# Five of the first eight expert weights issued in one block behind the output projection of a mixer and expert layer

## The reference

```python
h = rmsnorm(x, g_norm1) * (1 + sc1) + sh1
x = x + gt1 * hybrid_mixer(h, ...)             # ends with  concatenate(...) @ w_out
h = rmsnorm(x, g_norm2) * (1 + sc2) + sh2
x = x + gt2 * moe(h, router_w, router_b, exp_w1, exp_w3, exp_w2)
return rmsnorm(x, g_final)

# moe: softmax of h @ router_w, 2 of 32 experts for each row, then for each expert
ys = (silu(xb @ w1[e]) * (xb @ w3[e])) @ w2[e]
```

## Time and profile before

| | us |
|---|---|
| median of 3 runs | 1104.49 (1103.25 to 1107.17) |
| the profiled execution's own time | 1103.69 |
| its span in the trace | 1101.9 |
| PE busy | 968.8 (88%) |
| DVE busy | 551.5 (50%) |
| ACT busy | 350.6 (32%) |
| all transfers | 295.82 MB, mean 268 GB/s |

### The profile page before, as it was taken

One profiled execution on the slowest core, in us unless ns is written; L12 is line 12 of the kernel. 1 busy time (PEld: TensorE's weight loads), 2 busy tenths in 40 slices (PEclk: granted clock), 3 DMA queues, 4 the chain that ended last, 5 costly groups with the idle time before them and its releaser, 6 DMA issues.

```text
span 1101.9 us, 12838 instructions
## 1 busy us (share of the span) xinstructions
PE 968.8 (88%) x4972; PEld 668.9 (61%) x4972; DVE 551.5 (50%) x848; ACT 350.6 (32%) x515; POOL 132.5 (12%) x131
## 2 busy tenths in 40 slices
PE   3799999999999799983999999999899989988810
PEld 2477888888889488872666546554554455444500
DVE  2588634523662256654873535453543354334547
ACT  5521024323222344322742425222423142234212
POOL 2000000001200002103031112020100102000112
PEclk9899899999999999985999999999999999999965
DMA  9829511111303263357989999999999999998665
GB/s 369 296 88 343 194 40 39 39 39 40 116 2 134 77 259 124 115 162 191 377 326 364 401 428 426 428 427 427 426 427 427 426 426 413 418 426 362 253 243 225
DMA packets 52271, 295.82 MB, mean 268 GB/s; under 512 B 10841, under 2 KB 23146, under 8 KB 35826
## 3 DMA queue, kind: packets, MB, share of 16 engines
q1 hardware_dynamic: 43634, 274.00, 63.0%
q0 software_dynamic: 7424, 16.80, 4.0%
q10 hardware_dynamic: 1152, 4.19, 0.9%
HBM read 278.03 MB, written 25.33 MB: 275 GB/s over the span
## 4 chain that ended last, share of the span: by engine, by line
PE 64%; DMA 19%; DVE 8%; ACT 4%; issue 2%; DVEq 1%; POOL 1%; SPq 0%; ACTq 0%; POOLq 0%
DMA place_dt_float<-in_exp_w_dram 14%; PE bank L1134 7%; PE bank L1115 7%; PE bank L1110 4%; PE bank L817 4%; PE bank L812 4%; PE bank L814 4%; PE bank L813 4%; PE bank L818 3%; PE bank L819 3%; PE bank L1104 3%; DVE place_dt_float32r L1928 3%; PE bank L1107 3%; PE bank L1140 2%; PE bank L986 2%; PE bank L992 2%
## 5 line engine op out<-in xcount | busy, mean ns | idle before, releaser
L1928 DVE TENSOR_TENSOR place_dt_float32r<-place_dt_float,place_dt_float32r 128x4096 fp32r<-128x4096 f32 x32 | 141.4, 4420 | 72.4 <-ACT place_dt_float32r L1398 72.4
L1398 ACT CAST place_dt_float32r<-place_dt_float 128x4096 fp32r<-128x4096 f32 x32 | 115.6, 3613 | 168.4 <-DMA place_dt_float<-in_exp_w_dram 146.8
L1115 PE MATMUL bank<-place_dt_float,tail_dt_float 128*64 128x512 f32 x512 | 113.4, 595 | 2.3 <-DMA place_dt_float<-in_exp_w_dram 2.3
L1134 PE MATMUL bank<-place_dt_float,arena 128*128 128x512 f32 x256 | 113.7, 597 | 1.7 <-issue 1.7
L713 POOL DMA_INDIRECT y_dram<-arena,slot_i x24 | 54.1, 2255 | 440.6 <-DVE arena L1939 440.6
L817 PE MATMUL bank<-low_r 128*128 128x256 f32 (+1 forms) x320 | 93.7, 293 | 0.0
L819 PE MATMUL bank<-low_r 128*128 128x256 f32 (+1 forms) x320 | 90.8, 284 | 0.0
L818 PE MATMUL bank<-low_r 128*128 128x256 f32 (+1 forms) x320 | 90.7, 284 | 0.0
L629 POOL TENSOR_TENSOR stats<-stats,half 128x1 f32<-128x1 f32 (+1 forms) x34 | 31.1, 918 | 467.7 <-DVE stats L1444 440.9
L1104 PE MATMUL bank<-place_dt_float32r,tail_dt_float32r 128*128 128x512 f32 x256 | 71.2, 422 | 15.4 <-ACT place_dt_float32r L1398 12.6
L812 PE MATMUL bank<-low_r 128*128 128x512 f32 x192 | 78.3, 408 | 5.0 <-DVE arena L1553 3.8
(11 more groups left out here) (263 smaller groups left out, 1510.5 us busy)
## 6 DMA issues: line engine op xcount, KB each, us to landing
place_dt_float<-in_exp_w_dram SPq DMA_DIRECT2D x96, 2048.0 KB, 28.3
arena<-in_w_ada_dram SPq DMA_DIRECT2D x24, 1024.0 KB, 9.3
low<-in_w_in_dram SPq DMA_DIRECT2D x11, 1024.0 KB, 5.6
arena<-y_dram SPq DMA_DIRECT2D x3, 2048.0 KB, 16.9
arena<-in_x_dram SPq DMA_DIRECT2D x2, 2048.0 KB, 12.3
wout_dt_float<-in_w_out_dram SPq DMA_DIRECT2D x2, 2048.0 KB, 8.0
arena<-in_x_dram SPq DMA_DIRECT2D x8, 512.0 KB, 3.5
x_dram<-arena SPq DMA_DIRECT2D x8, 512.0 KB, 3.9
```

The lines of the kernel that those rows point to most:

```text
L1115: mm = pe.matmul(out_[rows_, :], x[:, k, rows_], w[:, k, :], start=(k == 0), stop=(k == KD - 1))
L1134: mm = pe.matmul(bank[5 + j][:], hT_sb[:, k, :], ws[0][:, k, cols], start=(k == 0), stop=(k == KF - 1))
L1398: act.copy(part_hi[0 if kind == "w1" else 1], alias[F32][n % SLOTS]).then_inc(S["w_hi"], 1)
L1928: TT(alias[F32R][n], alias[F32][n], part_hi[j].bitcast(F32), ALU.subtract).then_inc(S["w_lo"], 1)
```

## The change

Units 6 and 7 are issued right behind units 3, 4 and 5, so that one loop issues the five. The wait for the gather of pass 1 (`gath[1]`), behind which they stood, is gone, and the load of the gate row `gt2` now stands behind all five. Nothing else is changed.

```diff
             sp.wait_ge(S["out_mm"], 2 * TILES)
             assert all(stream[n][2] < FIXED for n in range(SLOTS))
-            for n in range(3, 6):
+
+            for n in range(3, SLOTS):
                 load_unit(n, stream[n][2])
             for h in range(2):
                 sp.wait_ge(x2_st[h], 32 * TH)
             sp.dma_start(gt2, broad(gate_dram[1:2, :])).then_inc(S["gt_ld"], 16)
-
-            sp.wait_ge(gath[1], 16)
-            for n in range(6, SLOTS):
-                load_unit(n, stream[n][2])
-
             sp.wait_ge(S["order_ready"], 1)
```

## The result

The change makes the kernel slower: a median of 1109.41 us (10 runs, 1108.51 to 1113.21) against 1105.22 us before (10 runs, 1102.10 to 1107.67). The ratio is 1.0045, with a 95% interval of 1.0031 to 1.0058, that is +5.0 us (3.4 to 6.4) on 1105. The forecast was 1108.9 us, with a range of 1104.0 to 1112.0 and a slip of 4.4 us.

A forecast was written before the change was run, and what follows sets the result against it. PE bounds the expert stage first, the weight stream its end. Removed wait 0, plus 4.4 (larger of gather 0's 4.4 and the gate row's 3.7), plus 0: 1108.1 from 1103.69, written as median 1108.9 us; range 1104.0 to 1112.0.

The forecast's parts named there:

- What bounds the stage: Expert stage: PE bounds it first, the weight stream at its end; the chain's first wait for a weight begins at 751.90.
- Removing the wait for gather 1 is worth 0: Units 6 and 7 issued before 519.20: no gain, since PE needs them tens of us later; other end -9.8 us.
- The third set of list writes is not delayed: List writes landing at 509.3, before gather 0: weights are in flight already, so more queued behind add 0.
- Gather 0 from 4.5 to 8.9 us: Gather 0, issued at 514.10 amid weights, lands at 523.0: +4.4 us, judged from gather 3; bounds 0 and +5.5.
- the 1.1 us taken off for its last packets: Gather 0's landing: 524.1 by gather 3's price, cut to 523.0 because its last packets have the engines to themselves.
- Gate row at 524.3 and hidden: Gate row behind all five units lands at 524.3, beside gather 0's larger slip, there when PE has transposed at 525.1.
- a floor of 3.7 us: Before DVE's first `x_evac`: the late gate row alone delays the first product about 3.7 us, even with a quick gather.
- My sign for the loads: Sign expected in the changed profile: DMA busy without a gap to 521, then idle until unit 8 near 535.
- Gathers pass in one go: Rival at gather 0: its packets go together, little delayed, so the gate row binds; +3.7 us, 1108.2; 8%.
- Hidden slip: Rival from the first product to the end: the stream catches up in gaps, absorbing part; +0 to +3 us; 17%.
- Full stream's price: Rival: gather 0 takes 11.8 to 15.7 us, or list writes stretch unit 7's tail; +7.3 to +11.2 us; 12%.
- The clock at the first products: PE's granted clock at the first products: low before and would be after, so 0 us.

The follow-up runs named there:

- late run: Kernel before, with units 6 and 7 issued behind the first product of pass 0 in place of gather 1; ratio 0.9991 to before.
- gate row between: The change, but with the gate row load between units 5 and 6 and not behind all five; ratio 1.0053 to before.
- halves: The change, with units 6 and 7 each loaded as two DMAs of half the columns (8 KB packets, not 16 KB), gate row last; ratio 1.0069 to before.
- none early: Kernel before, with units 3 to 7 all behind the wait for gather 1 and only the gate row ahead; ratio 1.0015 to before.
- two early: Kernel before, with only units 3 and 4 ahead of the gate row, units 5 to 7 behind gather 1; ratio 0.9987 to before, 0.9989 when repeated.
- one unit: Kernel before, with only unit 6 joining units 3 to 5 and unit 7 staying behind gather 1; ratio 1.0013 to before.
- halves with the gate row between: The change, with units 6 and 7 as two half-column DMAs each and the gate row between units 5 and 6; ratio 1.0029 to before.
- halves with lists later: The change with units 6 and 7 as half-column DMAs, gate row last, and the last list writes issued behind gather 2, not gather 1; ratio 1.0040 to before.

## Why the prediction was right

**What bounds the stage: right.** PE's chain from the first product on, then the stream from 752. The chain's first wait for a weight moved from 751.90 to 760.02, with the first product.

**Removing the wait for gather 1 is worth 0: right.** Units 6 and 7 issued twelve us later cost nothing (-2.7 to +0.7 us), so there was no lack of room that landing them some 11 and 13 us earlier (519.1 and 523.9 against 529.9 and 537.0) could have filled; and with one of them early the time didn't fall either. It holds only as long as the queue runs empty before 620.

**The third set of list writes is not delayed: right, as far as the scatter lets one see.** From its last issue it took 11.03 us before and 10.00 in the late run, with three units ahead; 10.84 with four; and 11.37 in the change, 10.75 with the gate row between and from 10.7 to 11.7 in the runs with halves, with five. What I passed over is that this landing, 1.9 us of DVE's waiting, was itself a cost of weights queued too early. That was the better lever on the same lines.

**Gather 0 from 4.5 to 8.9 us: right in kind, 0.6 too small.** It took 9.47 and 9.69 us with both units ahead. The term that was too small is the 1.1 us taken off for its last packets; unit 7 landed at 523.9, not at 522.6. I had carried the price over from gather 3 without parting it. The runs part it: 2.4 of the 5.0 us pass behind the first packet and shrink with the weights' packets, as turns would make them do, and 2.5 pass before the first packet, for which I had no account. That the sum came so near is thus in part luck.

**Gate row at 524.3 and hidden: right.** It landed at 525.9, 0.6 us ahead of need. I had counted a floor of 3.7 us from it and no more; how thin that margin was the halves showed, where list writes pushed it to 528.5 and it became the bound. I had no rival for that. My sign for the loads was out of step with my own sum: I wrote that they would be busy to 521, but the sum had unit 7 at 522.6 and the gate row at 524.3. Their last packets moved at 525.5.

**Gathers pass in one go:** the rule of packets of many descriptors ("DMA: Bandwidth & Descriptors", "Queues, rings and completion order", in the Trainium skill) would have let gather 0 through together. The trace differs: equal counts of packets on both queues, 46 and 46, then 105 and 105, speak for turns of a single packet of the trace between these two queues.

**Hidden slip: wrong.** In the trace the slip of 8.0 us at 549.67 is 8.1 at 760.02, and the median took +5.0 (3.4 to 6.4) of the first product's 5.35. **Full stream's price: wrong.** The gather was below 10 us in every run with five units.

**The clock at the first products: 0 assumed.** For the median that was good enough; between single executions it is worth 2.5 us (below).

## What to carry to other kernels

A prefetch is free only for the one who waits for it. Look at which small transfer on the critical chain is issued while it is in flight: a small gather (gathers 0 and 1 move 0.25 MB together) lost 5.0 us with 3.3 MB of loads still queued, most of which nobody needed for tens of us, and 1.4 us with 1.4 MB. Ask whether the transfer queue runs empty between here and the point where it becomes the bound: as long as it does, large loads can be placed later at no cost that these runs could measure, out of the way of gathers, list writes and gate rows. Once it doesn't, a late start is paid at the end: with none early a first product 1.7 us sooner became a time 1.7 us longer.

## What the runs showed of the hardware

- Beside small writes the other queue is slow. While a set of 4-byte list writes drains beside weights, both together move at 195 GB/s over 10 us where 427 is usual. No run takes the writes out of that stretch with the weights left in it, so that they are the cause is argued, not shown. Taking them away from the end of the loads, with halves, brought a landing forward by 3.3 us.
- A gather's first packet comes 1.7 us after the issue with nothing queued and 4.2 us after it beside queued weights, whether their packets are 16 KB or 8 KB. What it waits for stays open.
- TensorE's granted clock around the start of the experts takes one of two courses. In seven of the eleven profiled executions (the change, gate row between, late, halves, none early and both of two early) the second product group takes 2.7 to 3.0 us, and the clock falls once more behind PE's next wait, to a mean of 0.72 in the 6 us around it. In the other four (before, one unit, halves with the gate row between, halves with lists later) the same group takes 1.8 to 2.1 us and the clock stays at 1.00. That is 2.5 us between the change and before. The 1.7 us at the very end come and go as well: the last `@ w2` takes 8.8 us in six of the eleven and 7.1 in five, among these the slower gate row between. Runs of one kernel spread by about as much (the late run's twelve lie in 1102.7 to 1103.3 and 1105.7 to 1107.5), which this may explain, but only one execution of each was profiled, so it is not shown.
